# A third feature pair by seven block products in the down projection, with the four extra banks kept in rows and spread once

## The chip, the cores and the metric

One core of a Trainium2 chip runs the whole program in one launch. The metric is the device time of one execution in microseconds; runs of this kernel agree within about 0.05%. TensorE multiplies, VectorE (DVE) and ScalarE (ACT) prepare operands and drain results, GpSimd (POOL) and SyncE (SP) mostly issue transfers.

## The reference, cut to what matters

Two transformer blocks over 256 tokens with 2048 features, in float32. The change lies in the feed-forward part at the end of the second:

```python
u = rms_norm(h, g_pre_mlp[l])
f = jnp.square(jax.nn.relu(u @ w_up[l])) @ w_down[l]    # 2048 -> 8192 -> 2048
h = h + rms_norm(f, g_post_mlp[l])
```

## The kernel before, in words

Every weight is split into a rounded high part and a low rest, and every product is three matmuls (high x high, high x low, low x high). The 8192 features of the feed-forward part go in four quarters: `w_up0` makes 2048 of them, `w_down0` multiplies them back and adds into `y_rows` [256 tokens x 2048], then `w_up1`, `w_down1` and so on. `w_up` yields its features in eight groups of 256, which is eight **pairs** of 128-feature tiles (0 to 7).

The weights come as a single stream of **slabs** of 512 KB for all stages. A slab of `w_down` holds one pair x 512 output columns; TensorE does 12 matmuls of 512 columns on it (2 feature tiles x 2 token tiles x 3). A step of `w_down0` to `w_down2` covers 1024 output columns in two parts of 512, one accumulator bank pair for each, so each pair appears twice in a step, once for each part. I call the places of a step's slabs **slots**, from 0.

For the pairs in `SEVENS` the 2 x 2 x 2 blocks (2 token tiles, 2 feature tiles, 2 column parts) are multiplied by a scheme with seven block products in place of eight: 21 matmuls in place of 24. Such a pair takes four slots, of which two load a weight slab (`LEFT`, `RIGHT`) and two hold sums of weight blocks (`OUTER`, `INNER`), made by VectorE in the stage ring (`weight_sums`, three operations, L541, L546 and L549). TensorE does 6, 3, 6 and 6 matmuls on the four (`seven_products`). The scheme needs sums of feature blocks too (`feature_sums`, five VectorE operations after the group of that pair, L2547 to L2551), and leaves four extra results in the four banks of `aux`, which have to be spread over the four output blocks.

The order around a slab is fixed. There are 8 stages for landed slabs and 4 pairs of buffers for split ones. SyncE loads slab n when slab n - 8 has been split. ScalarE rounds slab n (`round_high`, L517) when TensorE is done with slab n - 4, VectorE subtracts (`subtract_low`, L531) after it, TensorE waits for the subtraction. The streams of ScalarE and VectorE are written as a loop over slots: at slot i each does its part of slab i + 4, then, if slot i closes a part, its drain (`down_body`: two additions into `y_rows`, L2566; `up_body`: the fold L742 and three more), then whatever stands `beside` slot i. Weight sums for a seven-product pair that begins in slot n stand ahead of the subtractions for slots n, n - 2 and n - 1. The banks of a part come free with its drain; slot 0 and slot 1 of a step open new banks and wait for `acc_free`.

In `w_down0` to `w_down2` the spread of the extra banks is done at each step: ScalarE copies the first bank (`z1_out`, L1447), VectorE does the rest straight from the banks (`sevens_out`, L2583 to L2598), and TensorE waits for `sevens_out` before it opens those banks again in the next step.

## Time and profile before

| | |
|---|---|
| median of 3 runs | 2041.9 us (2041.61 to 2042.46) |
| profiled execution | 2042.42 us, of it span 2040.6 us |
| TensorE matmuls | 2027.5 us busy (99%), 10536 |
| VectorE | 1442.1 us (71%), 1945 instructions |
| ScalarE | 970.1 us (48%), 1255 |
| GpSimd | 80.7 us (4%), 91 |
| mean transfer rate | 191 GB/s |

The span runs from the first to the last instruction; what the execution took beyond it lies around the program. Matmuls overlap in the view, so that a length in it is not the spacing of two matmuls. Busy shares are means over all stages; what counts for a change is which wait ends last in its own stage.

### The profile page before, as it was taken

The page shows a single profiled execution, that of the slowest core. Times are in us where ns is not written, and L with a number is a line of the kernel's source. Part 1 is how long each engine was busy: PE and PEld are TensorE (multiplying, and loading weights), DVE is VectorE, ACT ScalarE, POOL GpSimd, SP SyncE. Part 2 cuts the span into 40 slices and gives each one's busy share as a digit, 9 for nine tenths or more (in the row PEclk, how much of TensorE's full clock was granted, in tenths as well). Part 3 has the DMA queues.
Part 4 walks back from the last instruction along what each step waited for, and adds up shares of the span by engine and source line. Part 5 has one row for each costly group of instructions (what it writes and reads, how often), then busy time and mean ns, then how long its engine had stood idle before and what let it go on. Part 6 is the DMA issues. An engine that isn't in the chain of part 4 may idle for free.

```text
span 2040.6 us, 28978 instructions
## 1 busy us (share of the span) xinstructions
PE 2027.5 (99%) x10536; PEld 1724.7 (85%) x10536; DVE 1442.1 (71%) x1945; ACT 970.1 (48%) x1255; POOL 80.7 (4%) x91
## 2 busy tenths in 40 slices
PE   9999999999999999999999999999999999999998
PEld 7888898888888888999888888888888888888886
DVE  6766766566756565678999856577767877877655
ACT  6645444565544444433444644553443443444343
POOL 0000102001001000002000000000000000000001
PEclk9999999999999999999999999999999999999999
DMA  9687656656677666555666676645675565566663
GB/s 349 195 202 186 178 156 178 182 167 180 186 216 229 187 187 187 175 175 157 190 192 201 180 234 187 206 149 173 196 222 180 183 213 184 165 205 207 194 194 105
DMA packets 265476, 389.33 MB, mean 191 GB/s; under 512 B 12505, under 2 KB 147033, under 8 KB 264572
## 3 DMA queue, kind: packets, MB, share of 16 engines
q1 hardware_dynamic: 262587, 377.19, 61.3%
q0 software_dynamic: 2624, 10.54, 1.9%
q8 instruction: 74, 1.21, 0.2%
q14 instruction: 47, 0.38, 0.1%
q10 hardware_dynamic: 144, 0.01, 0.0%
HBM read 385.02 MB, written 2.54 MB: 190 GB/s over the span
## 4 chain that ended last, share of the span: by engine, by line
PE 96%; DVE 2%; SPq 1%; DMA 1%; ACT 0%; issue 0%; DVEq 0%; ACTq 0%
PE acc L700 18%; PE acc L677 18%; PE acc L679 17%; PE acc L678 17%; PE acc L698 10%; PE acc L692 2%; PE acc L690 2%; PE acc L691 2%; PE acc L696 1%; PE aux L1602 1%; DVE low_rows L531 1%; PE aux L1686 1%; PE aux L725 1%; PE aux L727 1%; PE aux L726 1%; DMA stage_rows<-in_w_mem_kv 1%
## 5 line engine op out<-in xcount | busy, mean ns | idle before, releaser
L531 DVE TENSOR_TENSOR low_rows<-stage_rows,high_rows 128x1024 fp32r<-128x1024 f32 x462 | 560.8, 1222 | 335.0 <-ACT high_rows L517 328.7
L517 ACT ACTIVATE high_rows<-stage_rows 128x1024 fp32r<-128x1024 f32 x462 | 481.2, 1047 | 554.3 <-PE acc L679 496.6
L517 ACT ACTIVATE w_high<-stage 128x1024 fp32r<-128x1024 f32 (+1 forms) x264 | 276.3, 1047 | 417.1 <-PE acc L700 298.9
L531 DVE TENSOR_TENSOR w_low<-stage,w_high 128x1024 fp32r<-128x1024 f32 (+1 forms) x264 | 320.8, 1221 | 211.6 <-ACT w_high L517 206.3
L700 PE MATMUL acc<-u,w_high 128*128 128x512 f32 x900 | 248.0, 394 | 0.0
L700 PE MATMUL acc<-hT,w_high 128*128 128x512 f32 x645 | 177.5, 394 | 0.0
L700 PEld LDWEIGHTS acc<-u,w_high 128*128 128x128 f32 x900 | 152.9, 189 | 19.1
L698 PEld LDWEIGHTS acc<-u,w_low 128*128 128x128 f32 x960 | 146.8, 188 | 20.5
L677 PE MATMUL acc<-high_rows,f_pair 128*128 128x512 f32 x400 | 156.4, 391 | 1.4 <-DVEq L2568 1.3
L679 PE MATMUL acc<-high_rows,f_pair 128*128 128x512 f32 x400 | 155.7, 389 | 0.0
L678 PE MATMUL acc<-low_rows,f_pair 128*128 128x512 f32 x400 | 155.7, 389 | 0.0
L698 PE MATMUL acc<-u,w_low 128*128 128x256 f32 x960 | 152.4, 281 | 0.0
L677 PE MATMUL acc<-high_rows,hT 128*128 128x512 f32 x384 | 151.8, 395 | 0.0
L679 PE MATMUL acc<-high_rows,hT 128*128 128x512 f32 x384 | 149.6, 390 | 0.0
L678 PE MATMUL acc<-low_rows,hT 128*128 128x512 f32 x384 | 149.6, 390 | 0.0
L700 PEld LDWEIGHTS acc<-hT,w_high 128*128 128x128 f32 x645 | 109.6, 189 | 13.4
L698 PEld LDWEIGHTS acc<-hT,w_low 128*128 128x128 f32 x688 | 104.0, 188 | 15.6 <-issue 2.7
L698 PE MATMUL acc<-hT,w_low 128*128 128x256 f32 x688 | 112.0, 285 | 0.0
L690 PE MATMUL acc<-uT,w_high 128*128 128x272 f32 x384 | 111.1, 289 | 0.0
L692 PE MATMUL acc<-uT,w_high 128*128 128x272 f32 x384 | 110.8, 288 | 0.0
L691 PE MATMUL acc<-uT,w_low 128*128 128x272 f32 x384 | 110.4, 288 | 0.0
L2305 DVE SCALAR_TENSOR_TENSOR conv<-glu,params,conv 128x256 f32<-128x256 f32 x240 | 108.0, 500 | 2.1 <-DVEq L2343 0.8
(454 smaller groups left out, 3498.4 us busy)
## 6 DMA issues: line engine op xcount, KB each, us to landing
stage_rows<-in_w_in SPq DMA_DIRECT2D x160, 512.0 KB, 3.9
stage<-in_w_in SPq DMA_DIRECT2D x136, 512.0 KB, 3.7
stage_rows<-in_w_down SPq DMA_DIRECT2D x128, 512.0 KB, 4.4
stage<-in_w_up SPq DMA_DIRECT2D x120, 512.0 KB, 4.1
stage_rows<-in_w_o SPq DMA_DIRECT2D x64, 512.0 KB, 4.2
stage_rows<-in_w_pool_out SPq DMA_DIRECT2D x16, 512.0 KB, 4.3
stage_rows<-in_w_conv_out SPq DMA_DIRECT2D x16, 512.0 KB, 4.7
stage_rows<-in_w_mem_kv SPq DMA_DIRECT2D x14, 512.0 KB, 11.4
```

What stands on the lines that cost most here:

```text
L517: act.activation(high[:, pr, k_from:kt, 0:p.cols], src[:, slot, k_from:kt, 0:p.cols], ACT.Copy).then_inc(high_done, 1)
L531: dve.tensor_tensor(low[:, pr, k_from:kt, 0:p.cols], src[:, slot, k_from:kt, 0:p.cols], high[:, pr, k_from:kt, 0:p.cols].bitcast(F32), ALU ...
L677: pe.matmul(bk, x_high, high, start=first, stop=False)
L678: pe.matmul(bk, x_high, low, start=False, stop=False)
L679: mm = pe.matmul(bk, x_low, high, start=False, stop=final)
L690: pe.matmul(dst, tile(w_high, k), b, start=first, stop=False)
L691: pe.matmul(dst, tile(w_low, k), a, start=False, stop=False)
L692: mm = pe.matmul(dst, tile(w_high, k), a, start=False, stop=final)
L696: pe.matmul(bk, tile(w_high, 0), p.rhs(0)[0], start=True, stop=False, skip_group_check=True)
L698: pe.matmul(bk[:, 0:T], tile(w_low, k), p.rhs(k0 + k)[1], start=False, stop=False, skip_group_check=True)
L700: mm = pe.matmul(bk, tile(w_high, k), p.rhs(k0 + k)[0], start=False, stop=last and k == kt - 1, skip_group_check=True)
L2305: ins = dve.scalar_tensor_tensor(out=conv[:, k, :], in0=glu[:, k, tap:tap + T], scalar=w, in1=conv[:, k, :], op0=ALU.mult, op1=ALU.add)
```

## The change

The pairs with seven products become 2, 4 and 6 (before: 2 and 5), in the slot order 0, 0, pair 2 (four slots), 1, 1, pair 4, 3, 3, pair 6, then 5 and 7 for each part: 22 slots in place of 20. The pairs that load are the same, so no byte of weight is added. Since a pair may now begin in the last stage of the ring, its sums can stand there in turned order (`turned`, `ends`).

The four extra banks are no longer spread at each step. ScalarE copies all four (`copy_z`), two after the last `INNER` slot (17) and two at slot 19. In quarter 0 the copies go to eight rows `z_rows` (four for each step), in quarters 1 and 2 to two buffers `z_out` in turn, and GpSimd's queue adds them into `z_rows` by a transfer (`accum_op=ALU.add`, 256 KB each, 16 in all). A copy waits until its buffer's last transfer has landed. TensorE waits for the copies before it opens the banks again. VectorE spreads `z_rows` over `y_rows` once, by 16 operations two at a time beside slots of `w_up3` (`z_spread`). The drains of quarter 0 are plain copies, since nothing stands in `y_rows` yet. `gain_rows` moves to where `f_sums` lies and is loaded in `w_up3`.

```diff
-SEVENS = (2, 5)
-SEVEN_ORDER = ((0,), (2,), (1,), (3,), (5,), (4,), (6, 7))
+SEVENS = (2, 4, 6)
+SEVEN_ORDER = ((0,), (2,), (1,), (4,), (3,), (6,), (5, 7))
...
-        gain_rows = at("gain_rows", Z + 40, [P, D])
+        gain_rows = at("gain_rows", Z + 32, [P, D])
...
-        f_raw = at("f_raw", Z + 80, [P, 4, P])
-        seven_u = at("seven_u", Z + 116, [P, ROW])
-        seven_v = at("seven_v", Z + 118, [P, ROW])
-        seven_w = at("seven_w", Z + 120, [P, ROW])
+        f_raw = at("f_raw", 72.25, [P, 4, P])
+        z_out = [at(f"z_out{b}", 72.25 + 2 * b, [P, ROW]) for b in range(2)]
+        z_at = ((Z + 44, Z + 46, Z + 80, Z + 82), (Z + 116, Z + 118, Z + 120, 80.75))
+        z_rows = [[at(f"z_rows{step}{b}", kb, [P, ROW]) for b, kb in enumerate(places)] for step, places in enumerate(z_at)]
...
+                ends = stage_tiles[:, left:left + 4:3, :] if left < right else stage_tiles[:, right + 1:left + 1:left - right - 1, :]
+                dve.tensor_tensor(stage_tiles[:, outer:outer + 2, :], ends,
                                   stage_tiles[:, right:right + 1, :].to_broadcast([P, 2, ROW]), ALU.add).then_inc(landed[(n + 2) % STAGES], 16)
...
+            turned = 1 if (n - 2) % STAGES == STAGES - 1 else 0
...
-                    pe.wait_ge(s("sevens_out"), step)
+                    pe.wait_ge(s("z_copied"), 4 * step)
...
-                        OUTER: [(0, sums[1], aux[:, 1, :], True), (1, sums[0], aux[:, 3, :], True)],
+                        OUTER: [(turned, sums[1], aux[:, 1, :], True), (1 - turned, sums[0], aux[:, 3, :], True)],
...
+            pool.wait_ge(s("gains_in"), 16)
+            for q in (1, 2):
+                for step in range(2):
+                    for b in range(4):
+                        copies = 4 * (2 * (q - 1) + step) + b
+                        pool.wait_ge(s("z_copied"), 8 + copies + 1)
+                        pool.dma_start(z_rows[step][b][:], z_out[b % 2][:], accum_op=ALU.add).then_inc(z_added[b % 2], 16)
+            pool.wait_ge(used, PAIRS + jobs["w_up3"].slab0)
             pool.dma_start(gain_rows[:], A["g_post_mlp_2"].partition_broadcast(P)).then_inc(s("gains_in"), 16)
...
+            def copy_z(q):
                 job = jobs[f"w_down{q}"]
                 inner = max(idx for idx, kind in enumerate(job.kinds) if kind == INNER)
 
                 def beside(n):
                     step, idx = n // job.S, n % job.S
-                    if idx == inner:
-                        if q * job.steps + step:
-                            act.wait_ge(s("sevens_out"), q * job.steps + step)
-                        act.wait_ge(used, PAIRS + job.slab0 + n + 1)
-                        act.activation(seven_u[:] if q else y_rows[:, 0, 2 * step * ROW:(2 * step + 1) * ROW], aux[:, 0, :], ACT.Copy).then_inc(s("z1_out"), 1)
+                    for b in {inner: (0, 1), inner + 2: (2, 3)}.get(idx, ()):
+                        act.wait_ge(used, PAIRS + job.slab0 + step * job.S + inner + 1)
+                        if q:
+                            copies = 4 * ((q - 1) * job.steps + step) + b
+                            if copies >= 2:
+                                act.wait_ge(z_added[b % 2], 16 * (copies // 2))
+                        act.activation(z_out[b % 2][:] if q else z_rows[step][b][:], aux[:, b, :], ACT.Copy).then_inc(s("z_copied"), 1)
                 return beside
...
-                        feature_sums(SEVENS.index(g), f.rearrange("p (b t) -> p b t", b=4))
+                        feature_sums(int(name[-1]), SEVENS.index(g), f.rearrange("p (b t) -> p b t", b=4))
...
+                if q == 2 and e == 0:
+                    dve.wait_ge(z_added[0], 16 * 4)
...
-                    if job.sevens:
-                        dve.wait_ge(dve_link, link.n)
                     for t in range(2):
                         v = y_rows[:, t, r * ROW:(r + 1) * ROW]
-                        dve.tensor_tensor(v, banks[:, t, :], v, ALU.add).then_inc(s("down"), 1)
+                        if q == 0:
+                            dve.tensor_copy(v, banks[:, t, :]).then_inc(s("down"), 1)
+                        else:
+                            dve.tensor_tensor(v, banks[:, t, :], v, ALU.add).then_inc(s("down"), 1)
...
-            def sevens_out(q):
-                job = jobs[f"w_down{q}"]
-                z1, z5, z6, z7 = (aux[:, b, :] for b in range(4))
-                inner = max(idx for idx, kind in enumerate(job.kinds) if kind == INNER)
-
-                def beside(n):
-                    step, idx = n // job.S, n % job.S
-                    y11, y21, y12, y22 = (y_rows[:, t, (2 * step + half) * ROW:(2 * step + half + 1) * ROW] for half in range(2) for t in range(2))
-                    if idx == inner:
-                        dve.wait_ge(used, PAIRS + job.slab0 + n + 1)
-                        dve.wait_ge(s("z1_out"), q * job.steps + step + 1)
-                        if q:
-                            link.put(dve.tensor_tensor(y11, z1, y11, ALU.add))
-                        link(dve.tensor_tensor(seven_u[:], seven_u[:] if q else y11, z6, ALU.subtract))
-                    if idx == inner + 1:
-                        if q == 0:
-                            link.put(dve.scalar_tensor_tensor(out=y12, in0=seven_u[:], scalar=-1.0, in1=z5, op0=ALU.mult, op1=ALU.subtract))
-                            link(dve.tensor_tensor(y21, seven_u[:], z7, ALU.add))
-                            link(dve.scalar_tensor_tensor(out=y22, in0=y21, scalar=-1.0, in1=z5, op0=ALU.mult, op1=ALU.subtract))
-                        else:
-                            link.put(dve.tensor_tensor(seven_w[:], seven_u[:], z5, ALU.add))
-                            link(dve.tensor_tensor(seven_v[:], seven_u[:], z7, ALU.add))
-                            link.put(dve.tensor_tensor(y12, y12, seven_w[:], ALU.subtract))
-                    if idx == inner + 3:
-                        if q:
-                            link.put(dve.tensor_tensor(y21, y21, seven_v[:], ALU.add))
-                            link(dve.tensor_tensor(seven_v[:], seven_v[:], z5, ALU.add))
-                            link(dve.tensor_tensor(y22, y22, seven_v[:], ALU.subtract))
-                        dve.sem_inc(s("sevens_out"), 1)
-                return beside
+            def z_spread(step, stage):
+
+                z1, z5, z6, z7 = z_rows[step]
+                y11, y21, y12, y22 = (y_rows[:, t, (2 * step + half) * ROW:(2 * step + half + 1) * ROW] for half in range(2) for t in range(2))
+                if stage == 0:
+                    link(dve.tensor_tensor(y11, y11, z1[:], ALU.add))
+                    link(dve.tensor_tensor(z6[:], z1[:], z6[:], ALU.subtract))
+                elif stage == 1:
+                    link(dve.tensor_tensor(z7[:], z6[:], z7[:], ALU.add))
+                    link(dve.tensor_tensor(z6[:], z6[:], z5[:], ALU.add))
+                elif stage == 2:
+                    link(dve.tensor_tensor(z5[:], z7[:], z5[:], ALU.add))
+                    link(dve.tensor_tensor(y12, y12, z6[:], ALU.subtract))
+                else:
+                    link(dve.tensor_tensor(y21, y21, z7[:], ALU.add))
+                    link(dve.tensor_tensor(y22, y22, z5[:], ALU.subtract))
+
+            def beside_up3(n):
+                if n in SPREAD_AT:
+                    if n == SPREAD_AT[0]:
+                        for b in range(2):
+                            dve.wait_ge(z_added[b], 16 * 8)
+                    z_spread(SPREAD_AT.index(n) // 4, SPREAD_AT.index(n) % 4)
...
-                splitting(f"w_up{q}", up_body(f"w_up{q}", 0 if q else 2), 3, beside=(beside_up0, lambda n: None, lambda n: None, None)[q])
-                splitting(f"w_down{q}", down_body(q), beside=sevens_out(q) if q < 3 else None)
+                splitting(f"w_up{q}", up_body(f"w_up{q}", 0 if q else 2), 3, beside=(beside_up0, lambda n: None, lambda n: None, beside_up3)[q])
+                splitting(f"w_down{q}", down_body(q))
```

VectorE at the passage from `w_up1` to `w_down1`, before: the last group but one ends with L2540, then come the weight sums for pair 2 (L541, L546, L549) between the subtractions L531, and the fold of the last group, L742.

```order
L2540 TENSOR_TENSOR f_pair<-tmp,f_pair 128x2x256
L541 TENSOR_TENSOR stage_rows<-stage_rows 128x1024
L531 TENSOR_TENSOR low_rows<-stage_rows,high_rows 128x1024
L546 TENSOR_TENSOR stage_rows<-stage_rows 128x512
L531 TENSOR_TENSOR low_rows<-stage_rows,high_rows 128x1024
L549 TENSOR_TENSOR stage_rows<-stage_rows 128x512
L531 TENSOR_TENSOR low_rows<-stage_rows,high_rows 128x1024
L531 TENSOR_TENSOR low_rows<-stage_rows,high_rows 128x512
L742 TENSOR_REDUCE tmp<-acc 128x512
```

The same place in the changed kernel (the first of the five operations of the feature sums, L2562, stands just ahead of these rows; L543, L548 and L551 are the weight sums, L532 the subtractions, L745 the fold):

```order
L2563 TENSOR_TENSOR f_raw<-f_raw,tmp 128x128
L2564 TENSOR_TENSOR f_raw<-tmp,f_raw 128x128
L2565 CAST f_sums<-f_raw 128x512
L2566 TENSOR_TENSOR f_sums<-f_raw,f_sums 128x512
L543 TENSOR_TENSOR stage_rows<-stage_rows 128x1024
L532 TENSOR_TENSOR low_rows<-stage_rows,high_rows 128x1024
L548 TENSOR_TENSOR stage_rows<-stage_rows 128x512
L532 TENSOR_TENSOR low_rows<-stage_rows,high_rows 128x1024
L551 TENSOR_TENSOR stage_rows<-stage_rows 128x512
L532 TENSOR_TENSOR low_rows<-stage_rows,high_rows 128x1024
L532 TENSOR_TENSOR low_rows<-stage_rows,high_rows 128x512
L745 TENSOR_REDUCE tmp<-acc 128x512
```

The feature sums for pair 6 now stand between the last group but one and the weight sums; those of pair 5 stood one group earlier, where they are now not made.

VectorE after the last fold of `w_up1`, before: subtractions for slots 4 to 7, then the sums for pair 5 between those for 8 to 10, the half subtraction for 11, and six more.

```order
L531 TENSOR_TENSOR low_rows<-stage_rows,high_rows 128x1024 x4
L541 TENSOR_TENSOR stage_rows<-stage_rows 128x1024
L531 TENSOR_TENSOR low_rows<-stage_rows,high_rows 128x1024
L546 TENSOR_TENSOR stage_rows<-stage_rows 128x512
L531 TENSOR_TENSOR low_rows<-stage_rows,high_rows 128x1024
L549 TENSOR_TENSOR stage_rows<-stage_rows 128x512
L531 TENSOR_TENSOR low_rows<-stage_rows,high_rows 128x1024
L531 TENSOR_TENSOR low_rows<-stage_rows,high_rows 128x512
L531 TENSOR_TENSOR low_rows<-stage_rows,high_rows 128x1024 x6
```

In the changed kernel the subtractions for slots 4 and 5 are followed at once by the sums for pair 4, which begins in slot 8, and after two more by those for pair 6:

```order
L532 TENSOR_TENSOR low_rows<-stage_rows,high_rows 128x1024 x2
L543 TENSOR_TENSOR stage_rows<-stage_rows 128x1024
L532 TENSOR_TENSOR low_rows<-stage_rows,high_rows 128x1024
L548 TENSOR_TENSOR stage_rows<-stage_rows 128x512
L532 TENSOR_TENSOR low_rows<-stage_rows,high_rows 128x1024
L551 TENSOR_TENSOR stage_rows<-stage_rows 128x512
L532 TENSOR_TENSOR low_rows<-stage_rows,high_rows 128x1024
L532 TENSOR_TENSOR low_rows<-stage_rows,high_rows 128x512
L532 TENSOR_TENSOR low_rows<-stage_rows,high_rows 128x1024 x2
L543 TENSOR_TENSOR stage_rows<-stage_rows 128x1024
L532 TENSOR_TENSOR low_rows<-stage_rows,high_rows 128x1024
```

So the large sum moved from between the subtractions for slots 7 and 8 to between those for 5 and 6, and a second one stands between 11 and 12.

ScalarE in the first step of `w_down1`, before: roundings L517 and the one copy of an extra bank, L1447.

```order
L517 ACTIVATE high_rows<-stage_rows 128x512
L517 ACTIVATE high_rows<-stage_rows 128x1024 x6
L1447 ACTIVATE seven_u<-aux 128x512
L517 ACTIVATE high_rows<-stage_rows 128x1024 x5
L517 ACTIVATE high_rows<-stage_rows 128x512
```

In the changed kernel: roundings L518 and four copies into two buffers, two roundings apart.

```order
L518 ACTIVATE high_rows<-stage_rows 128x512
L518 ACTIVATE high_rows<-stage_rows 128x1024 x6
L1460 ACTIVATE z_out_134<-aux 128x512
L1460 ACTIVATE z_out_135<-aux 128x512
L518 ACTIVATE high_rows<-stage_rows 128x1024 x2
L1460 ACTIVATE z_out_134<-aux 128x512
L1460 ACTIVATE z_out_135<-aux 128x512
L518 ACTIVATE high_rows<-stage_rows 128x1024
L518 ACTIVATE high_rows<-stage_rows 128x512
```

The third copy writes the buffer of the first again, two roundings later.

## Rows read from the trace of the kernel before

**Rows 1.** The page, chain that ended last: shares by engine.

```profile
PE 96%; DVE 2%; SPq 1%; DMA 1%; ACT 0%; issue 0%; DVEq 0%; ACTq 0%
```

**Rows 2.** Waits of TensorE from 700 us on: waiting, releaser, us, times, longest.

```profile
PE acc L677 <- DVEq L2568: 1.3, 2, 0.7
```

**Rows 3.** Windows `w_down1`, `w_up3`: us, busy PE, PEld, DVE, ACT, POOL, clock, DMA.

```profile
1595.20:1680.90 85.70, 85.04 (x374) 69.73 (x373) 68.83 (x76) 41.25 (x42) 0.00 (x0) 1.00 0.67 211
1856.20:1945.90 89.70, 89.70 (x514) 78.40 (x513) 60.05 (x63) 33.95 (x32) 0.00 (x0) 1.00 0.60 189
```

**Rows 4.** The page's groups: busy us, mean ns | idle before.

```profile
L677 PE MATMUL acc<-high_rows,f_pair 128*128 128x512 f32 x400 | 156.4, 391 | 1.4 <-DVEq L2568 1.3
```

**Rows 5.** Timeline of TensorE, `w_down1`, slots 2 and 6: start, us.

```profile
1600.98 0.39 PE L725 MATMUL aux<-high_rows,f_pair 128*128 128x512 f32 x1
...
1605.74 0.39 PE L677 MATMUL acc<-high_rows,f_pair 128*128 128x512 f32 x1
```

**Rows 6.** Timeline of TensorE at slot 1 of three steps.

```profile
1465.49 0.39 PE L679 MATMUL acc<-high_rows,f_pair 128*128 128x512 f32 x1
1465.92 0.50 PE L677 MATMUL acc<-high_rows,f_pair 128*128 128x512 f32 x1
...
1597.74 0.39 PE L679 MATMUL acc<-high_rows,f_pair 128*128 128x512 f32 x1
1598.10 0.50 PE L677 MATMUL acc<-high_rows,f_pair 128*128 128x512 f32 x1
...
1640.19 0.39 PE L679 MATMUL acc<-high_rows,f_pair 128*128 128x512 f32 x1
1641.23 0.50 PE L677 MATMUL acc<-high_rows,f_pair 128*128 128x512 f32 x1 [0.66 <-DVEq L2568]
1641.57 0.40 PE L678 MATMUL acc<-low_rows,f_pair 128*128 128x512 f32 x1
```

**Rows 7.** Timeline of VectorE, end of `w_up1`; brackets: idle before, releaser.

```profile
1578.41 0.42 DVE L2547 TENSOR_TENSOR f_raw<-tmp 128x256 f32<-128x256 f32 x1
...
1580.59 3.49 DVE L531 TENSOR_TENSOR w_low<-stage,w_high 128x1024 fp32r<-128x1024 f32 x3
...
1594.29 1.22 DVE L531 TENSOR_TENSOR low_rows<-stage_rows,high_rows 128x1024 fp32r<-128x1024 f32 x1
1596.16 0.69 DVE L531 TENSOR_TENSOR low_rows<-stage_rows,high_rows 128x512 fp32r<-128x512 f32 x1 [0.65 <-ACT high_rows L517]
1596.77 1.22 DVE L742 TENSOR_REDUCE tmp<-acc 128x512 f32<-128x1024 f32 x1
```

**Rows 8.** Timeline of ScalarE and VectorE, `w_down1`, roundings and subtractions from slot 5.

```profile
1601.23 1.06 ACT L517 ACTIVATE high_rows<-stage_rows 128x1024 fp32r<-128x1024 f32 x1 [1.95 <-PE acc L679]
1602.60 3.10 ACT L517 ACTIVATE high_rows<-stage_rows 128x1024 fp32r<-128x1024 f32 x3 [0.30 <-PE acc L727]
...
1602.33 3.73 DVE L531 TENSOR_TENSOR low_rows<-stage_rows,high_rows 128x1024 fp32r<-128x1024 f32 x3 [1.18 <-ACT high_rows L517]
1605.97 1.22 DVE L541 TENSOR_TENSOR stage_rows<-stage_rows 128x1024 f32<-128x1024 f32 x1
```

**Rows 9.** Timeline of VectorE, end of the first step of `w_down1`.

```profile
1633.35 0.69 DVE L2598 TENSOR_TENSOR y_rows<-y_rows,seven_v 128x512 f32<-128x512 f32 x1
...
1639.84 1.28 DVE L2566 TENSOR_TENSOR y_rows<-acc,y_rows 128x512 f32<-128x512 f32 x2
```

**Rows 10.** Timeline of ScalarE after the last seven-product slot.

```profile
1621.63 1.06 ACT L517 ACTIVATE high_rows<-stage_rows 128x1024 fp32r<-128x1024 f32 x1 [0.30 <-PE acc L727]
1622.60 0.58 ACT L1447 ACTIVATE seven_u<-aux 128x512 f32<-128x512 f32 x1
```

**Rows 11.** Transfers: KB each, median us to landing; last `bias_ring` alone.

```profile
bias_ring<-in_gate_bias POOLq DMA_DIRECT2D x12, 256.0 KB, 4.1
toep<-bias_rows POOLq DMA_DIRECT2D x8, 288.0 KB, 9.5
...
DMA to landing us min/median/max: 3.6/4.1/5.6
```

More of the change, by code:

```diff
@@ L477, in build @@
         stream_of_slabs = [(job, step, idx) for _, job in order for step in range(job.steps) for idx in range(job.S)]
+        SPREAD_AT = (5, 8, 11, 14, 17, 20, 23, 26)
+        z_added = [sem(f"z_added{b}") for b in range(2)]
         SUMS_BEFORE = {}
@@ L545, in weight_sums @@
                 dve.wait_ge(split_done, n + 3 + 1)
-                dve.tensor_tensor(stage_tiles[:, inner, :], stage_tiles[:, outer, :], stage_tiles[:, right + 1, :], ALU.add).then_inc(s("inner_sum"), 1)
+                dve.tensor_tensor(stage_tiles[:, inner, :], stage_tiles[:, outer if left < right else outer + 1, :], stage_tiles[:, right + 1, :], ALU.add).then_inc(s("inner_sum"), 1)
             else:
@@ L1451, in _ @@
                 rounding(f"w_up{q}", beside=beside_up0 if q == 0 else None)
-                rounding(f"w_down{q}", last_down if q == 3 else None, beside=z1_out(q) if q < 3 else None)
+                rounding(f"w_down{q}", last_down if q == 3 else None, beside=copy_z(q) if q < 3 else None)
         @block.tensor
@@ L2447, in mixed_body @@
                 if r == 0:
-                    dve.wait_ge(s("gains_in"), 32)
+                    dve.wait_ge(s("gains_in"), 16)
                 for t in range(2):
@@ L2541, in body, with feature_sums @@
                     if name != "w_up3" and g in SEVENS:
-                        feature_sums(SEVENS.index(g), f.rearrange("p (b t) -> p b t", b=4))
+                        feature_sums(int(name[-1]), SEVENS.index(g), f.rearrange("p (b t) -> p b t", b=4))
                 return body
-            def feature_sums(e, f):
+            def feature_sums(q, e, f):
+                if q == 2 and e == 0:
+                    dve.wait_ge(z_added[0], 16 * 4)
                 link(dve.tensor_tensor(f_raw[:, 0:2, :], f[:, 0:4:3, :], f[:, 1:2, :].to_broadcast([P, 2, P]), ALU.subtract))
```

3 lines of the change are left out of this document (removed).

## The prediction

> **What bounds the kernel now.** I read the page first: the chain that ended last is TensorE for 96% of the span [rows 1], so a change counts only by what it takes from TensorE or makes it wait. The waits of TensorE come next: all those it has in the second half of the program are on the drain of accumulator banks in `w_down`, 1.3 us in two places [rows 2]. The windows by stage then show how much room the others have: in `w_down1` TensorE is busy 85.04 of 85.70 us, VectorE already 68.83, ScalarE 41.25 and GpSimd nothing; in `w_up3` VectorE is busy 60.05 of 89.70 [rows 3]. So TensorE sets the pace, and VectorE is near enough to it that its order decides where TensorE waits.
>
> **What a matmul is worth.** The table of groups gives 391 ns for one 512-column matmul [rows 4]. That is its length, not its spacing. The 21 matmuls of the first seven-product pair of `w_down1` start at 1600.98, and the next slab starts at 1605.74: 4.76 us, 0.227 us each [rows 5]. An ordinary slab of 12 takes 2.72 us. The change turns 24 matmuls of a pair into 21 in each of 3 quarters x 2 steps: 18 fewer, **-4.1 us** (by the length it would be -7.0, which is not what the engine gives back). The Trainium skill (TensorE: Matmul & The Clock Gate, Back-to-back issue gap) puts a sustained stream of 512-column matmuls at about 131 ns each; by that page's figure the gain would be 2.4 us and an estimate of the sum made with it 1.7 us worse than mine. The trace has 227 ns in this very code, and the sum uses that.
>
> **What TensorE waits for now.** At slot 1 of each step of `w_down` it needs a bank pair that VectorE has to drain. Between `w_up1` and `w_down1` the last matmul of slot 0 starts at 1597.74 and the next at 1598.10: 0.36 instead of 0.23, a stall of 0.14; the first interval after a stall is 0.34 instead of 0.23 (1641.23 to 1641.57), so each stall costs 0.11 more. Between the two steps the stall is 1.05 - 0.23 = 0.82 in `w_down1` (`w_down2` has the same) and 0.43 - 0.23 = 0.20 in `w_down0` [rows 6]. With the 0.11 each, the three step boundaries cost 2.2 us now.
>
> **Third set of feature sums.** Pairs 2 and 5 become 2, 4 and 6. The five small operations for pair 6 come after the fold of group 6, one group before the end of `w_up`, and behind them stand the block sums of the weights for the first seven-product pair and the last fold, for which slot 1 of `w_down` waits. The five take 2.18 us of VectorE (1578.41 to 1580.59). In that stretch VectorE has only one pause, before the half subtraction at 1596.16: its predecessor leaves the issue slot 1.14 us after 1594.29, so 0.73 us are free (0.65 as the view counts idle time). The fold at 1596.77 comes 2.18 - 0.73 = 1.45 us later, and TensorE is already waiting for it [rows 7]. That gives **+4.35 us** over three quarters. Only a longer pause than this one could hide it, and the rows show none; if the sums cost nothing at all (no row says so) it would be 0.
>
> **Third set of weight sums, in the middle of a step.** Three more VectorE operations (1.22, 0.69, 0.69 us) per step replace nothing in time, since they belong to slots that load nothing. Their number is small against the step; their place matters. Before, the first seven-product pair is followed by four ordinary slabs, so the sums of the next come when TensorE is at slots of 2.72 us. Now only two ordinary slabs lie between, and the large sum for the next pair stands between the subtractions for slots 5 and 6, while TensorE does slots that last 0.68 to 1.36 us. With the times of `w_down1`: VectorE can start slot 5's subtraction at 1602.33, when ScalarE's rounding (1601.23 + 1.06) is in. VectorE issues such operations every (3.49 - 1.22) / 2 = 1.14 us [rows 7]. Sum at 1603.47, subtraction for slot 6 at 1604.61, done 1605.83. ScalarE isn't the limit: its three roundings from 1602.60 have the first ready by 1603.66. TensorE wants slot 6 at 1605.74 [rows 5, 8]. A hand-over takes 0.04 (1602.29 to 1602.33), so it stalls 0.12 and pays the 0.11: 0.23. The same figure stands again at slot 12, and both in 6 steps: **+2.8 us** for twelve. This is a narrow one: were the subtraction 0.12 us earlier it would be nothing, and if the sums for later operands come 0.3 us later still, it is 6.4 us. I take 2.8, by the rows.
>
> **Work removed from the end of a step.** The spreading of the four extra banks by VectorE (eight operations of about 0.68 us per step in quarters 1 and 2) leaves `w_down`; three of these stand in a row at its end, until 1633.35 + 0.69 = 1634.04, ahead of the sums and the two drains, the last of which begins only at 1639.84 and lets TensorE on at 1641.23 [rows 6, 9]. In the new order, from the end of slot 19 (t = 0): rounding in at 1.2, subtraction, drain to 3.6, the small sum 3.7, the next subtraction 4.3; the half subtraction waits for slot 21 and its rounding (5.44 + 0.1 + 0.63 = 6.2), drain done 8.1, bank free 8.2. TensorE would reach slot 1 at 3 x 2.72 - 0.16 = 8.0 (0.16 is the part of a matmul that overlaps the next). Stall 0.2 + 0.11 = 0.3, so 0.9 for three boundaries instead of 2.2: **-1.3 us**. If all of it went away it would be -2.2, if nothing changed 0.
>
> **Four copies by ScalarE, adding transfers by GpSimd.** A copy of a bank takes 0.58 us; today there is one per step [rows 10], now four: two after the last seven-product slot, two two slots later. ScalarE is busy half the time and the next rounding has room, so the copies are free by themselves. But in quarters 1 and 2 the third copy reuses the buffer of the first, whose transfer must have landed. From the start of the rounding at 1621.63: first copy ends 1.55, transfers issued at about 1.65 and 2.2, slot 19's rounding ends at 6.5, then copies 3 and 4 wait until 1.65 + L and 2.2 + L, with L the time from issue to landing. Behind them stand the roundings for the next slots, then the subtractions, then the drain above. By the chain of the last part TensorE feels nothing while L is under about 6.5 us; from there each us of L costs one us at the step boundary of `w_down1` and of `w_down2`: 2 x (L - 6.5). The trace has no adding transfer. Nearest rows, also through GpSimd's queue and of 256 KB: 4.1 us, 3.6 to 5.6. The far one is `toep`, 288 KB in small pieces, 9.5 [rows 11]. The added read of the destination puts it above 4.1, and I take about 5: **0 us**; at 9.5 it is +6.0, and less than 0 it can't be. The Trainium skill (DMA: Bandwidth & Descriptors, Anatomy of one DMA) gives 2.0 us plus bytes over 436 GB/s for this path, 2.6 us for 256 KB; the rows here have 4.1 for that size, so I don't lean on it, and by it too TensorE would see nothing.
>
> **The spread at the end** is 16 VectorE operations of 0.69 us in `w_up3`, 11 us in a stage where VectorE has 29.6 us free [rows 3], two at a time next to a single fold deadline: 0. Uncovered it would be 11 us, but only if those 29.6 us of pauses weren't there. Drains in quarter 0 become plain copies and the load of `gain_rows` moves to `w_up3`, some 80 us before its use: 0.
>
> **Sum:** -4.1 + 4.35 + 2.8 - 1.3 = +1.75 us. The profiled execution took 2042.42 us (span 2040.6), 0.5 above the median of the runs; on the median, 2041.9, this gives **2043.7 us**. What can be told from no change is about 0.2%, 4.1 us.
>
> **Rivals.**
> - *The stalls at slots 6 and 12 don't come* (the narrow one above): -4.1 + 4.35 - 1.3 = -1.05, 2040.9 us. For it: it hangs on 0.12 us. Chance 0.15.
> - *Faster*: neither these nor the late fold come, since VectorE would have room that I don't see: -4.1 - 1.3 = -5.4, 2036.5 us. It decides when the pause ahead of the last fold is over 2.2 us; the rows have 0.73. Chance 0.06.
> - *The adding transfers are late*: L of 8 us gives +3 on top (2046.7), 9.5 gives +6 (2049.7). It decides the sign at L over about 7.7. For it: a read and a write per element and weight loads beside it; against it 3.6 to 5.6 in the nearest row. Chance 0.17, and 0.03 for a mild form that stays within 0.2%.
> - *VectorE falls behind in the dense part of the step*: slots 2 to 17, three seven-product pairs and four ordinary slabs, need 3 x 6.4 + 4 x 1.14 = 23.8 us of its time (a pair: four operations at 1.14, three at 0.60) against 3 x 4.76 + 4 x 2.72 = 25.2 of TensorE's. If each of the twelve stalls is 0.3 longer: +3.6, 2047.3 us. Chance 0.07.
> - The forecast itself: 0.52.
>
> **How the numbers follow.** 2043.7 is the likeliest case. The range of 8 in 10 takes in the first rival, and above the forecast the late transfers up to L near 8.5: 2040.4 to 2048.0. Faster by over 0.2%: 0.06. Slower by over 0.2%: 0.17 + 0.07 = 0.24. Within: 0.52 + 0.15 + 0.03 = 0.70.
>
> **What would show each step.** 18 fewer matmuls, still 0.227 apart. TensorE's gap at slot 1 of each `w_down` step 0 of about 1.6 us, waiting for the fold; at slots 6 and 12 gaps of 0.1 with the subtraction as what ended them; at the step boundary 0.2 instead of 0.8. The adding transfers' issue to landing near 5 us, and ScalarE waiting under 1 us for them. The three quarters should each end about 0.6 us later against before. Wrong makes it a landing over 7 us, a fold that isn't late, or a VectorE backlog that grows through a step.

## The result, and the profile after

The changed kernel took 2052.3 us (median of 7 runs; before 2041.7 in the same session): ratio 1.0048, 95% interval 1.0037 to 1.0059, about 10 us slower. The forecast was 2043.7, with 2048.0 as the upper end. The execution that was profiled with it took 9121.8 us at a mean granted clock of 0.21 (the other six have a median of 2051.8), so the profile shown here is that of the same kernel in a second session (2051.6 us, ratio 1.0044, 1.0031 to 1.0058), at a mean granted clock of 0.998.

Its page: span, TensorE and the chain that ended last, to be held against [rows 1].

```profile
span 2049.8 us, 28965 instructions
PE 2028.0 (99%) x10518; PEld 1722.6 (84%) x10518; DVE 1457.6 (71%) x1966; ACT 988.1 (48%) x1285; POOL 94.5 (5%) x107
PE 95%; DVE 3%; DMA 1%; ACT 1%; issue 0%; SPq 0%; DVEq 0%; POOL 0%; ACTq 0%
```

TensorE has its 18 matmuls fewer (10536 to 10518) and is still nearly the whole chain. So the loss is in what it waits for. The windows before and from 1340 us (columns as in [rows 3]), first of the kernel before, then of the changed one:

```profile
1340.00:2040.60 700.60, 691.60 (x3487) 585.74 (x3485) 511.73 (x565) 299.53 (x320) 7.66 (x6) 1.00 0.60 186
```

```profile
1340.00:2049.80 709.80, 691.94 (x3473) 582.34 (x3471) 528.20 (x588) 318.45 (x351) 22.05 (x23) 1.00 0.62 191
```

9.2 us more. (1.0 of it was lost ahead of `w_down0`: the first matmul on `f_pair` starts at 1421.5 instead of 1420.5. It comes back below, with "The rest of the 6.05".) The waits of TensorE from 1340 us, which answer to [rows 2], name the two places:

```profile
PE acc L679 <- DVEq L2584: 4.8, 2, 3.1
PE acc L679 <- DVEq L2548: 4.2, 3, 1.4
PE acc L679 <- DVE low_rows L532: 0.4, 1, 0.4
```

L2584 is the drain at a step boundary, L2548 the last fold of `w_up`. The timeline of TensorE shows them beside the stall at slot 6, in `w_down1`, as [rows 6] did:

```profile
1600.17 0.39 PE L681 MATMUL acc<-high_rows,f_pair 128*128 128x512 f32 x1
1601.97 0.50 PE L679 MATMUL acc<-high_rows,f_pair 128*128 128x512 f32 x1 [1.41 <-DVEq L2548]
...
1609.36 0.39 PE L730 MATMUL acc<-high_rows,f_pair 128*128 128x512 f32 x1
1609.82 0.47 PE L679 MATMUL acc<-high_rows,f_pair 128*128 128x512 f32 x1
1610.13 0.40 PE L680 MATMUL acc<-low_rows,f_pair 128*128 128x512 f32 x1
...
1611.98 0.39 PE L679 MATMUL acc<-high_rows,f_pair 128*128 128x512 f32 x1
...
1644.07 0.39 PE L681 MATMUL acc<-high_rows,f_pair 128*128 128x512 f32 x1
1647.58 0.50 PE L679 MATMUL acc<-high_rows,f_pair 128*128 128x512 f32 x1 [3.12 <-DVEq L2584]
```

At slot 1 of step 0 the matmuls start 1.80 us apart, in each of the three quarters; at slots 6 and 12 0.46 (once 0.75, at slot 12 of the first step of `w_down2`), then 0.31; at the step boundary 3.51 in `w_down1`, 2.03 in `w_down2` and 0.43 in `w_down0`. The late fold is the one forecast. VectorE at the end of `w_up1`, as in [rows 7]:

```profile
1592.12 0.42 DVE L2562 TENSOR_TENSOR f_raw<-tmp 128x256 f32<-128x256 f32 x1
...
1594.29 1.22 DVE L543 TENSOR_TENSOR stage_rows<-stage_rows 128x1024 f32<-128x1024 f32 x1
...
1598.90 1.82 DVE L532 TENSOR_TENSOR low_rows<-stage_rows,high_rows 128x1024 fp32r<-128x1024 f32 x2
1600.64 1.22 DVE L745 TENSOR_REDUCE tmp<-acc 128x512 f32<-128x1024 f32 x1
```

The five sums take 1592.12 to 1594.29, and from there to the fold VectorE doesn't pause. The step boundary is not the one forecast. ScalarE around the four copies of the first step of `w_down1` (brackets: idle before, releaser), which answers to [rows 10]:

```profile
1631.93 1.07 ACT L1460 ACTIVATE z_out<-aux 128x512 f32<-128x512 f32 x2
1633.68 1.06 ACT L518 ACTIVATE high_rows<-stage_rows 128x1024 fp32r<-128x1024 f32 x1 [0.69 <-PE acc L681]
1636.40 1.06 ACT L518 ACTIVATE high_rows<-stage_rows 128x1024 fp32r<-128x1024 f32 x1 [1.66 <-PE acc L681]
1640.37 0.60 ACT L1460 ACTIVATE z_out<-aux 128x512 f32<-128x512 f32 x1 [2.92 <-DMA z_rows<-z_out]
1642.86 0.60 ACT L1460 ACTIVATE z_out<-aux 128x512 f32<-128x512 f32 x1 [1.89 <-DMA z_rows<-z_out]
1643.36 2.51 ACT L518 ACTIVATE high_rows<-stage_rows 128x1024 fp32r<-128x1024 f32 x3
```

The third copy waits for the first transfer until 1640.37, the fourth for the second until 1642.86, and three roundings stand behind it in a heap. GpSimd issued the two from 1633.08, the second from 1633.66 (second line), and VectorE, idle for 3.62 us, could drain only from 1646.18 (compare [rows 9]):

```profile
1633.08 1.80 POOL L905 DMA_DIRECT2D z_rows<-z_out  x2 [438.59 <-ACT z_out L1460]
...
1633.66 1.22 POOL L905 DMA_DIRECT2D z_rows<-z_out  x1
```

```profile
1644.44 1.83 DVE L532 TENSOR_TENSOR low_rows<-stage_rows,high_rows 128x1024 fp32r<-128x1024 f32 x2 [3.62 <-ACT high_rows L518]
1646.18 1.28 DVE L2582 TENSOR_TENSOR y_rows<-acc,y_rows 128x512 f32<-128x512 f32 x2
```

Over all 16 adding transfers, the tile's view (the second line: us from issue to landing, to be held against [rows 11]):

```profile
  DMA z_rows<-z_out: 16.7, 8
...
DMA to landing us min/median/max: 3.6/6.8/9.1
```

So the first theory: the landing, not 5 us but 6.8 and up to 9.1, costs the largest part of the loss, through the two buffers. Its rivals: the adding transfers are innocent and the dense part of the step or the third pair costs it; or it is the late fold alone.

### The profile page after: what moved, and what is told of

It is laid out like the page before. It is cut to its first block, busy times and chain, and to the rows that moved or that the text cites. A ratio compares the mean times of both kernels' runs of the same rounds, so it can differ in the third digit from the quotient of the medians.

```text
span 9120.0 us, 28965 instructions
## 1 busy us (share of the span) xinstructions
PE 9108.0 (100%) x10518; PEld 6833.8 (75%) x10518; DVE 1468.5 (16%) x1966; ACT 995.8 (11%) x1285; POOL 92.5 (1%) x107
## 4 chain that ended last, share of the span: by engine, by line
PE 99%; SPq 0%; DMA 0%; DVE 0%; ACT 0%; issue 0%; DVEq 0%
PE acc L679 19%; PE acc L681 19%; PE acc L680 19%; PE acc L702 15%; PE acc L700 8%; PE acc L694 3%; PE acc L693 3%; PE acc L692 3%; PE aux L730 1%; PE aux L729 1%; PE aux L728 1%; PE acc L698 1%; PE acc L728 1%; PE acc L729 1%; PE acc L730 1%; PE aux L1699 1%
## 5 line engine op out<-in xcount | busy, mean ns | idle before, releaser
L532 DVE TENSOR_TENSOR low_rows<-stage_rows,high_rows 128x1024 fp32r<-128x1024 f32 x474 | 571.5, 1207 | 4886.3 <-ACT high_rows L518 4883.6
L702 PE MATMUL acc<-u,w_high 128*128 128x512 f32 x900 | 1278.0, 1694 | 0.0
L518 ACT ACTIVATE high_rows<-stage_rows 128x1024 fp32r<-128x1024 f32 x474 | 492.1, 1040 | 5051.2 <-PE acc L681 4299.1
L700 PEld LDWEIGHTS acc<-u,w_low 128*128 128x128 f32 x960 | 757.6, 916 | 195.4 <-issue 195.4
L702 PEld LDWEIGHTS acc<-u,w_high 128*128 128x128 f32 x900 | 764.2, 918 | 168.4 <-issue 168.4
L700 PE MATMUL acc<-u,w_low 128*128 128x256 f32 x960 | 723.3, 1033 | 0.0
L532 DVE TENSOR_TENSOR w_low<-stage,w_high 128x1024 fp32r<-128x1024 f32 (+1 forms) x264 | 320.5, 1214 | 2450.8 <-ACT w_high L518 2447.9
L681 PE MATMUL acc<-high_rows,f_pair 128*128 128x512 f32 x352 | 596.5, 1695 | 0.0
L680 PE MATMUL acc<-low_rows,f_pair 128*128 128x512 f32 x352 | 596.3, 1694 | 0.0
L679 PE MATMUL acc<-high_rows,f_pair 128*128 128x512 f32 x352 | 596.0, 1693 | 0.0
L518 ACT ACTIVATE w_high<-stage 128x1024 fp32r<-128x1024 f32 (+1 forms) x264 | 275.8, 1045 | 2687.2 <-PE acc L702 1657.4
L679 PE MATMUL acc<-high_rows,uT 128*128 128x512 f32 x256 | 435.3, 1701 | 0.0
L681 PE MATMUL acc<-high_rows,uT 128*128 128x512 f32 x256 | 433.9, 1695 | 0.0
L679 PEld LDWEIGHTS acc<-high_rows,f_pair 128*128 128x128 f32 x352 | 321.9, 915 | 144.2 <-issue 144.2
L681 PEld LDWEIGHTS acc<-high_rows,f_pair 128*128 128x128 f32 x352 | 321.5, 913 | 143.8 <-issue 143.8
L679 PE MATMUL acc<-high_rows,hT 128*128 128x512 f32 x384 | 417.9, 1088 | 0.0
L681 PE MATMUL acc<-high_rows,hT 128*128 128x512 f32 x384 | 414.4, 1079 | 0.0
L692 PE MATMUL acc<-uT,w_high 128*128 128x272 f32 x384 | 413.5, 1077 | 0.0
L694 PE MATMUL acc<-uT,w_high 128*128 128x272 f32 x384 | 413.4, 1077 | 0.0
```

What stands on the lines that cost most here:

```text
L518: act.activation(high[:, pr, k_from:kt, 0:p.cols], src[:, slot, k_from:kt, 0:p.cols], ACT.Copy).then_inc(high_done, 1)
L532: dve.tensor_tensor(low[:, pr, k_from:kt, 0:p.cols], src[:, slot, k_from:kt, 0:p.cols], high[:, pr, k_from:kt, 0:p.cols].bitcast(F32), ALU ...
L679: pe.matmul(bk, x_high, high, start=first, stop=False)
L680: pe.matmul(bk, x_high, low, start=False, stop=False)
L681: mm = pe.matmul(bk, x_low, high, start=False, stop=final)
L692: pe.matmul(dst, tile(w_high, k), b, start=first, stop=False)
```

## The experiments

The kernel before had a median of 2042.1 to 2042.5 us in these sessions. The intervals given are about 2 us or more to either side, so differences of 1 us between two experiments rest on their traces.

**1. The changed kernel again.** No edit.

> The changed kernel once more, for a profile at full clock. Theory T (late transfers): the 16 adding transfers land about 10 us after their issue while the weight loads run (the forecast took 5), ScalarE's third copy waits for them, and TensorE stands some 3.5 to 4 us at slot 1 of the second step of w_down1 and of w_down2; the rest is as forecast (1.6 us at slot 1 of each first step, 0.1 to 0.2 at slots 6 and 12). Rival V (VectorE's backlog in the dense part): landing 5 to 6 us, no long gap at the step boundary, and gaps of 0.7 to 0.9 us at slots 6 and 12 of all six steps. Both: 2051.5 us, about +9.7 on the kernel before.

2051.6 us (2048.9 to 2054.5). Its trace is the one above. The loss stands; its 5 runs lie 5.6 us apart, 24 of the kernel before 2.2 (0.1%, twice the agreement named at the start). The theory holds in kind, not in size: the transfers landed after 3.6 to 9.1 us, not 10, and of the two long gaps (less the 0.23 of a matmul) only that of `w_down1` is near the expected 3.5, with 3.3; that of `w_down2` is 1.8.

**2. Four copy buffers.** `z_out` gets two more, so that no copy waits for a transfer of its own step.

```diff
-        z_out = [at(f"z_out{b}", 72.25 + 2 * b, [P, ROW]) for b in range(2)]
+        z_out = [at(f"z_out{b}", kb, [P, ROW]) for b, kb in enumerate((72.25, 74.25, 68, 70))]
...
-                            if copies >= 2:
-                                act.wait_ge(z_added[b % 2], 16 * (copies // 2))
+                            if copies >= 4:
+                                act.wait_ge(z_added[b], z_base[b] + 16 * (copies // 4))
...
```

> The changed kernel with four copy buffers in place of two, so that a copy waits for the transfer four copies back (a whole step earlier) and never for one just issued; transfers, copies, spread and slot order unchanged. T: 2043.7 us (about +2 on the kernel before), the step boundary gap falls to 0.3. V: unchanged, 2051.5.

2045.5 us (2044.8 to 2046.0), ratio 1.0015 (1.0006 to 1.0024): 6.05 us less than experiment 1. The transfers are no faster, but nothing waits for them. Landings, then TensorE at the boundary of `w_down1`:

```profile
DMA to landing us min/median/max: 6.3/7.7/9.2
```

```profile
1642.27 0.39 PE L682 MATMUL acc<-high_rows,f_pair 128*128 128x512 f32 x1
1642.70 0.50 PE L680 MATMUL acc<-high_rows,f_pair 128*128 128x512 f32 x1
```

0.43 us from start to start, where the forecast had a stall of 0.2 (0.43 with the 0.23 of a matmul). The landing wait is shown as the cause of this part. The time is 1.8 above the expected 2043.7; the stalls at slots 6 and 12, which cost more than forecast, are most of that (see below).

**3. The third pair is pair 5, not pair 6**, so that the feature sums come a group earlier.

```diff
-SEVENS = (2, 4, 6)
-SEVEN_ORDER = ((0,), (2,), (1,), (4,), (3,), (6,), (5, 7))
+SEVENS = (2, 4, 5)
+SEVEN_ORDER = ((0,), (2,), (1,), (4,), (3,), (5,), (6, 7))
```

> The changed kernel with pairs 2, 4 and 5 in place of 2, 4 and 6 (slot order 0, 2, 1, 4, 3, 5, then 6 and 7): the last feature sums come one group earlier, all else is the same. The late fold is worth 1.45 us in each quarter by the forecast: 4.4 us less than e1_again, 2047.1, and the gap at slot 1 of the first step of each w_down falls from 1.6 to 0.14. If the fold isn't late for that reason: as e1_again.

2047.7 us (2046.7 to 2048.6), ratio 1.0025 (1.0015 to 1.0036): 3.9 less than experiment 1, and the gap at slot 1 is 0.36 to 0.37 again. VectorE has its pause ahead of the last fold back, with the 0.65 of [rows 7]:

```profile
1595.83 0.69 DVE L532 TENSOR_TENSOR low_rows<-stage_rows,high_rows 128x512 fp32r<-128x512 f32 x1 [0.65 <-ACT high_rows L518]
1596.43 1.22 DVE L745 TENSOR_REDUCE tmp<-acc 128x512 f32<-128x1024 f32 x1
```

The long gap at the boundary stayed (3.48 us), and in this execution something follows it that experiment 1 didn't show. TensorE, then the window behind the gap (the 1.00 of the rows above, the granted clock, is 0.55 here):

```profile
1639.89 0.39 PE L681 MATMUL acc<-high_rows,f_pair 128*128 128x512 f32 x1
1643.37 0.50 PE L679 MATMUL acc<-high_rows,f_pair 128*128 128x512 f32 x1 [3.09 <-DVEq L2584]
...
1644.94 0.63 PE L680 MATMUL acc<-low_rows,f_pair 128*128 128x512 f32 x1
1645.37 0.63 PE L681 MATMUL acc<-high_rows,f_pair 128*128 128x512 f32 x1
```

```profile
1643.40:1647.00 3.60, 3.60 (x9) 2.87 (x10) 1.23 (x1) 0.00 (x0) 0.00 (x0) 0.55 0.26 69
```

Matmuls 0.43 us apart instead of 0.227: the clock is at 1.2 GHz, the lower of its levels. Nine of them in 3.6 us instead of 2.0: some 1.5 us on top of the wait.

**4. Both: four buffers and pair 5.**

> Both edits together. T: 1.75 - 4.4 = -2.6 on the kernel before, 2039.2 us. V: 2047. This is also the first candidate to beat the kernel before.

2041.4 us (2040.9 to 2042.5), ratio 0.9997 (0.9988 to 1.0006): 4.1 less than experiment 2, 6.3 less than experiment 3. The two causes add. It is 2.2 above what was expected, again mostly by the stalls: what is left over are the twelve stalls of 0.46 and 0.31 at slots 6 and 12.

**5. Weight sums a slot earlier** for the second and third pair, on top of 4.

```diff
-                        SUMS_BEFORE.update({n - 2: (OUTER, n), n - 1: ("first_inner", n), n: (INNER, n)})
+                        first = n - (1 if idx > 2 else 0)
+                        SUMS_BEFORE.update({first - 2: (OUTER, n), first - 1: ("first_inner", n), first: (INNER, n)})
...
```

> e4 (four buffers, pairs 2, 4 and 5) with the weight sums of the second and third seven-product pair of a step made one slot earlier, ahead of the subtraction for which VectorE waits anyway. Same work, other place. If the stalls at slots 6 and 12 are the large sum standing between two subtractions (0.31 us each in e1 and e4, twelve of them): 3.7 us less than e4, about -5 on the kernel before, 2037.2. If they are VectorE's total load in the dense part: the stalls move to other slots and the time stays at e4's 2041.4.

2040.1 us (2039.1 to 2040.6), ratio 0.9988 (0.9979 to 0.9997), 1.3 less than 4. The gap at slot 6 is gone, that at slot 12 has grown to 0.54 to 0.57 in five of the six steps (0.40 in the other), and at slot 11 one of 0.28 to 0.40 is new in three of them. A view of VectorE in `w_down1` says why: the sum for the third pair now stands so early that its weights haven't landed.

```profile
1611.53 1.23 DVE L545 TENSOR_TENSOR stage_rows<-stage_rows 128x1024 f32<-128x1024 f32 x1 [1.26 <-DMA stage_rows<-in_w_down]
```

**6. Two pairs as before, in the new way of spreading, four buffers.** `SEVENS` and `SEVEN_ORDER` are those of the kernel before.

> The new way with the extra banks (copies, adding transfers, one spread, four buffers) with the pairs and the slot order of the kernel before (2 and 5): no third pair. If deferring the spread gives only the step boundaries back: -1.3 us on the kernel before, 2040.9. If the copies and transfers cost something beside the landing wait: 2042 or more. The difference to e4 is what the third pair is worth.

2041.0 us (2040.6 to 2042.4), ratio 0.9995 (0.9986 to 1.0004). All three boundaries are at 0.43 us, and no other gap is left but the 0.36 at slot 1. Experiment 4 is 0.4 above it: as the order stood, the third pair gave nothing, its 4.1 us went into the twelve stalls.

**7. Plain copies as transfers.** The addition into `z_rows` is left out, so that each transfer overwrites them.

```diff
-                        pool.dma_start(z_rows[step][b][:], z_out[b % 2][:], accum_op=ALU.add).then_inc(z_added[b % 2], 16)
+                        pool.dma_start(z_rows[step][b][:], z_out[b % 2][:]).then_inc(z_added[b % 2], 16)
```

> The changed kernel with its 16 transfers as plain copies: the addition into z_rows is left out (the last quarter's extra banks alone remain), all waits stay. If it is the adding that makes them late: landing falls from 6.8 us (median in e1) to about 4 and the time by some 5 us, to 2046. If it is the queue beside the weight loads or the path itself: landing stays at 6 to 7 us and the time at 2051.

2046.4 us (2045.5 to 2046.9), ratio 1.002 (1.0011 to 1.003), 5.2 less than experiment 1. The transfers of the same bytes over the same queue (first line: GpSimd's time to issue one; last: issue to landing):

```profile
L905 POOL DMA_DIRECT2D z_rows<-z_out x16: 537/538/558, 1631.7 to 1859.2; - x16
...
  DMA z_rows<-z_out: 6.6, 7
...
DMA to landing us min/median/max: 3.1/5.0/6.7
```

The gaps at the boundaries are 0.74 and 0.77, near the forecast's 0.43 plus what the slowest landing (6.7) adds. The forecast's 5 us were meant for the adding transfer: 4.1 of the nearest row and 0.9 for the addition. Measured, the plain transfer takes 5.0, and the addition 1.8 us more to land and 0.32 more to issue (0.86 against 0.54).

**8. The kernel before, with pairs 2, 4 and 5 and its own spread.** It also takes over the turned order of the sums and the new place and time of `gain_rows` from the changed kernel.

```diff
-SEVENS = (2, 5)
-SEVEN_ORDER = ((0,), (2,), (1,), (3,), (5,), (4,), (6, 7))
+SEVENS = (2, 4, 5)
+SEVEN_ORDER = ((0,), (2,), (1,), (4,), (3,), (5,), (6, 7))
...
```

> The kernel before with pairs 2, 4 and 5 and the slot order 0, 2, 1, 4, 3, 5, then 6 and 7, but with its old spread at every step straight from the banks: the third pair alone. The spread then stands right behind the dense part, so that the drains at the end of a step come later: gaps of about 3 us at the three step boundaries, 0.3 at slots 6 and 12, +5 to +6 us on the kernel before, 2047.5. If VectorE has the room for it: -4.1 + 3.7 = about -0.4, 2041.8.

2051.9 us (2050.0 to 2056.7), ratio 1.0043 (1.0029 to 1.0057). Worse than expected. TensorE waits six times for the drain, 8.8 us (two gaps at each boundary, 1.76 and 1.22, 0.54 and 3.38, 0.55 and 3.72, where one of 3 was expected), and in the profiled execution, the slowest of the five (2056.7 us), after the two longest gaps its clock falls again, for longer:

```profile
PE acc L677 <- DVEq L2570: 8.8, 6, 3.3
```

```profile
1646.40:1653.40 7.00, 6.09 (x14) 4.79 (x15) 2.02 (x3) 0.50 (x1) 0.00 (x0) 0.51 0.27 75
```

14 matmuls in 6.1 us instead of 3.2, twice. The other four executions have a mean granted clock of 0.999 against its 0.994 and lie at 2050.0 to 2052.2, so these falls aren't in the median. In this order of slots the third pair costs 9.8 us with the old spread; the new one, with four buffers, is worth 10.5 us to it (experiment 4), though only 1.15 to two pairs (experiment 6).

**9. Sums for the second pair a slot earlier, the large sum for the third a slot later** (and with it the first small one), on top of 4 (`at`: the slots of the three sums, counted from where the pair begins).

```diff
-                        SUMS_BEFORE.update({n - 2: (OUTER, n), n - 1: ("first_inner", n), n: (INNER, n)})
+                        at = {2: (-2, -1, 0), 8: (-3, -2, -1), 14: (-1, 0, 0)}[idx]
+                        for where, what in zip(at, (OUTER, "first_inner", INNER)):
+                            SUMS_BEFORE.setdefault(n + where, []).append((what, n))
...
```

> e4 (four buffers, pairs 2, 4 and 5) with the second pair's weight sums one slot earlier and the third pair's large sum one slot later (ahead of the subtraction for slot 13, the two small ones together ahead of that for slot 14). e5 had both earlier, and its trace shows VectorE waiting up to 1.3 us for the landing of slot 15's slab at the third pair. If place is all: no stall at slots 6, 10 or 12, 12 x 0.31 = 3.7 us less than e4, some -5 on the kernel before, 2037. If the load as such holds VectorE back: no better than e5's 2040.05.

2036.9 us (2036.2 to 2038.6), ratio 0.9973 (0.9963 to 0.9984): 4.5 less than experiment 4, and faster than both kernels. No gap is left at slots 6 and 12. In the changed kernel VectorE had the sum between the subtractions for slots 5 and 6; here it stands ahead of both (the 1.22 at L543 of the first, at L546 of the second fence; the last line of each is the subtraction for slot 6). It is done 0.44 us before TensorE's first matmul of slot 6, at 1603.70 (third fence), where that of the changed kernel ended at 1609.67, after the 1609.59 at which that matmul was due:

```profile
1606.18 1.23 DVE L532 TENSOR_TENSOR low_rows<-stage_rows,high_rows 128x1024 fp32r<-128x1024 f32 x1 [1.15 <-ACT high_rows L518]
1607.32 1.22 DVE L543 TENSOR_TENSOR stage_rows<-stage_rows 128x1024 f32<-128x1024 f32 x1
1608.45 1.22 DVE L532 TENSOR_TENSOR low_rows<-stage_rows,high_rows 128x1024 fp32r<-128x1024 f32 x1
```

```profile
1599.04 1.22 DVE L546 TENSOR_TENSOR stage_rows<-stage_rows 128x1024 f32<-128x1024 f32 x1
1600.30 1.22 DVE L535 TENSOR_TENSOR low_rows<-stage_rows,high_rows 128x1024 fp32r<-128x1024 f32 x1
...
1602.04 1.22 DVE L535 TENSOR_TENSOR low_rows<-stage_rows,high_rows 128x1024 fp32r<-128x1024 f32 x1
```

```profile
1603.70 0.39 PE L682 MATMUL acc<-high_rows,f_pair 128*128 128x512 f32 x1
```

The window of the second part answers to the two shown with the result, 5.9 us below the kernel before:

```profile
1340.00:2034.70 694.70, 686.88 (x3466) 581.90 (x3464) 527.24 (x585) 317.08 (x350) 22.15 (x23) 1.00 0.63 195
```

**10. The large sum a slot later for both pairs**, `8: (-1, 0, 0)` in the same place.

> As e9, but the second pair's large sum one slot later too (ahead of the subtraction for slot 7). If the stall hangs only on what stands ahead of the subtraction for the slot right after a seven-product pair (6 and 12): as e9, 2037. If the later sums press on the roundings of slots 10 and 16: new stalls there, 2039 or more.

2037.1 us (2036.4 to 2038.3), ratio 0.9973 (0.9962 to 0.9984), the same as experiment 9. Either way around the subtraction for slot 6 is enough.

## Why the prediction was wrong

**The step that failed** is the last price of "Four copies by ScalarE, adding transfers by GpSimd: 0 us", the landing time L. L was taken at 5 us, nearer to the 4.1 of the nearest row than to the far 9.5. The trace has 6.8 in the median, but what counts is the slower of the two transfers that follow each other, since the fourth copy waits for it: the two of `w_down1` land after 7.2 and 9.1 us (issued at 1633.08 and 1633.66), those of `w_down2` after 6.1 and 8.0. The text had the mechanism, the threshold of 6.5 us and the slope; it gave the case where the transfers are late 0.17. By its rule the two boundaries would cost 2.6 and 1.5 us at L = 9.1 and 8.0; they cost 3.51 - 0.43 = 3.1 and 2.03 - 0.43 = 1.6, together 4.7 us, against the 0 of the forecast. Removing the wait gave 6.05 us back (experiments 1 and 2). Three things are in it: the plain transfer is slower than its nearest row (5.0, not 4.1), the addition takes 1.8, and the second of two in a row lands 1.5 to 1.9 later than the first, which the forecast didn't price. The Trainium skill (DMA: Bandwidth & Descriptors, Anatomy of one DMA) has 2.0 us plus bytes over 436 GB/s, an estimate of 2.6 us for this size. It was further off than the rows: even the plain copy took 5.0.

**The rest of the 6.05** is open. From the first matmul on `f_pair` to the end the traces of experiments 1 and 2 are 628.3 and 623.3 us long, 5.0 apart: the 4.7 at the boundaries, and 0.3 of the gap of 0.75 at a slot 12. Their spans lie 6.8 apart (2049.8 and 2043.0); the other 1.8 stand ahead of `w_down0`, where both do the same work. There, in experiment 1, TensorE pauses for 2.35 us (from start to start) and then has half the clock, 1.2 GHz, for 3.4 us:

```profile
11.79 0.39 PE L681 MATMUL acc<-high_rows,mem_pair 128*128 128x512 f32 x1
14.14 0.74 PE L679 MATMUL acc<-high_rows,mem_pair 128*128 128x512 f32 x1 [1.97 <-DVE low_rows L532]
```

```profile
14.20:17.60 3.40, 3.40 (x8) 2.71 (x9) 2.88 (x4) 2.76 (x5) 0.00 (x0) 0.50 1.03 397
```

The traces of experiments 1 and 8 have this fall and reach `f_pair` at 1421.4 to 1421.5; the other nine don't have it and are there at 1419.7 to 1420.7. So the 1.0 us lost ahead of `w_down0` in the profile shown isn't a price of the third pair. The forecast had no term for the clock at all: it priced each microsecond of waiting at one. At the step boundary the clock cost 1.5 us in the trace of experiment 3 and nothing in that of experiment 1. For the executions without a trace there is only the mean granted clock: 0.999 in 6 of the 19 of the kernels that wait for a landing at a gap of over 3 us (the changed one in both sessions, without the one at 0.21, and experiment 3; the others 0.997 and 0.998), and in 68 of the 69 of experiments 2, 4 to 7, 9 and 10. So the clock most likely has a part in the 1 us of the medians that the traces leave over; no run tells how much of it, or at which of the two places.

**Fewer matmuls, -4.1**: right. Experiment 9 is experiment 6 with a third pair and without stalls of its own, and 4.05 us lie between them (4.0 in the traces, from the first matmul on `f_pair` to the end).

**Third feature sums, +4.35**: right. 1.80 - 0.36 = 1.44 us a quarter in the trace, 4.3 in all; moving them a group earlier gave 3.9 and 4.1.

**Third weight sums, +2.8**: the mechanism was right to the slot, and the size too small, the second term that was mis-sized. The wait and the first interval make 0.23 + 0.08 = 0.31, not 0.23, and the next few matmuls are slower too: the ten intervals from 1609.36 to 1611.98 take 2.62 us instead of 2.27. Between experiments 4 and 9, which differ only in where the sums stand, the traces lie 4.3 us apart (619.0 and 614.8, counted as above) and the medians 4.5: 0.36 a stall, **4.3 us** for twelve. The case that they don't come is refuted, though it took only one operation's change of place to make it so.

**Work removed from the end of a step, -1.3**: right where the landing doesn't cover it. All boundaries are at 0.43 us in experiments 2, 4 and 6, and experiment 6 is 1.15 us below the kernel before (1.3 in the traces, counted as above).

**Copies by themselves, the spread in `w_up3`, plain drains: 0**: nothing in the traces speaks against it; experiment 2 is 2045.5, and the terms without the landing wait, with stalls at their measured size, give 2042.2 - 4.1 + 4.3 + 4.3 - 1.3 = 2045.4.

**VectorE falls behind**: no. The stalls don't grow through a step; they are 0.46 and 0.31 at both places.

**The sum of the changed kernel's trace**, with the boundaries at 2.46 + 0.99 = +3.4 against [rows 6] instead of -1.3: -4.1 + 4.3 + 4.3 + 3.4 = +7.9 us of the 8.2 lost from `w_down0` on. The gap of 0.75 instead of 0.46 at one slot 12 is the other 0.3; the traces of experiments 3 and 7 have it at the same place, none with four buffers has it, and its cause isn't shown.

## What to carry to other kernels

When a buffer is handed back by a transfer, the landing time is a term of the sum and wants a price from above: it was cheaper to make the wait impossible with two more buffers (6 us) than to have its mean right, and two transfers in a row land later than one. When a helper operation has to go into a dense stretch of an order, count which operand is needed next and put the helper ahead of it by two or behind it: the same sums in a neighbouring slot made the difference between a third pair that gives nothing and one that gives its whole 4.1 us. And a wait of some us on TensorE may cost more than its length: in some executions, not in all, its clock fell after gaps of 2.35 to 3.72 us.

## What the hardware showed that I had not expected

- A 256 KB transfer that adds, from SBUF to SBUF through GpSimd's queue beside the weight loads, took 6.8 us from issue to landing in the median (3.6 to 9.1), a plain one 5.0 (3.1 to 6.7); issuing took 0.86 and 0.54 us of the queue. In experiment 1, of two issued in a row the first landed after 6.1 to 7.5 us and the second after 8.0 to 9.1; those issued alone took 3.6 to 6.9.
- TensorE's granted clock fell to the lower of its two levels after gaps of 3.38, 3.48 and 3.72 us from start to start (experiments 8, 3, 8) and stayed at 1.00 after one of 3.51 (experiment 1). Near 12 us of the span it fell after 2.35 and 2.44 us (experiments 1 and 8) and stayed after 2.55 and 2.56 (experiments 3 and 10). So the length of a gap alone didn't decide it. The Trainium skill (TensorE: Matmul & The Clock Gate, Part 1) says that the clock goes to its lower level when the engine has idled; the five falls agree, and the three other gaps show that lengths like these needn't do it.
- A stall costs more than its wait: the interval after the first matmul was 0.34 us after a wait for a bank and 0.31 after a wait for an operand, where 0.227 is the rule, and after the latter the next few were 0.23 to 0.24.
